# One low part of the next expert's gate weights, moved ahead of the scaling of finished rows

## The reference

```python
# each token goes to 2 of 32 experts; rows are sorted by expert, in blocks
def run_block(args):
    xb, e = args
    h = jax.nn.silu(xb @ w_gate[e]) * (xb @ w_up[e])     # 1024 -> 512
    return h @ w_down[e]                                  # 512 -> 1024
out = out.at[slot_tok].add(ys * slot_gate[:, None])
x = x + out
return rms_norm(x, final_g)        # x * rsqrt(mean(x*x) + eps) * g, row by row
```

## Time and profile before

| what | value |
| --- | --- |
| median of the runs | 2077.36 us (2075.55 to 2087.81, 3 runs) |
| the profiled execution, its own time | 2084.54 us |
| span of the profiled execution | 2082.6 us |
| granted clock over the span | 0.971 |
| PE busy | 1935.8 us, 93% |
| DVE busy | 1344.3 us, 65% |
| ACT busy | 1166.8 us, 56% |
| POOL busy | 868.4 us, 42% |

### The profile page before, as it was taken

How to read it: one execution, slowest core, us unless ns; L and a number is a source line. 1 busy time by engine, 2 the same in 40 slices (tenths; PEclk the granted TensorE clock), 3 DMA queues, 4 the chain that set the end, 5 groups by cost and what they waited for, 6 DMA issues and landing times. The chain is left out here.

```text
span 2082.6 us, 39849 instructions
## 1 busy us (share of the span) xinstructions
PE 1935.8 (93%) x12329; PEld 1646.0 (79%) x12330; DVE 1344.3 (65%) x2479; ACT 1166.8 (56%) x2436; POOL 868.4 (42%) x1044
## 2 busy tenths in 40 slices
PE   7999999979999999989999679899999999999996
PEld 6888888867777787878878568788888888788885
DVE  5333333339888888845656559766777777787764
ACT  4211111128888889853333248666666667686763
POOL 3332222213656644431332335445454345344544
PEclk9999999979999999989999889999999999999998
DMA  7433334375363543224543569968878978987852
GB/s 224 147 122 122 121 121 123 114 187 151 107 189 98 131 112 92 69 72 152 166 167 126 209 197 368 359 219 295 288 267 289 361 243 292 364 300 288 287 196 71
DMA packets 230803, 406.35 MB, mean 195 GB/s; under 512 B 31201, under 2 KB 169057, under 8 KB 206480
## 3 DMA queue, kind: packets, MB, share of 16 engines
q1 hardware_dynamic: 201328, 352.08, 49.7%
q0 software_dynamic: 29376, 53.03, 9.6%
HBM read 345.83 MB, written 111.15 MB: 219 GB/s over the span
## 5 line engine op out<-in xcount | busy, mean ns | idle before, releaser
L747 ACT ACTIVATE prob<-score,nmax 128x512 f32<-128x512 f32 (+3 forms) x464 | 264.4, 580 | 24.7 <-DVE nmax L897 24.1
L65 PE MATMUL proj<-w_in_lo,n1T_hi 128*128 128x512 f32 (+1 forms) x640 | 242.8, 379 | 3.5 <-DVE w_in_lo L250 3.4
L897 DVE TENSOR_REDUCE nmax<-score 128x2 f32<-128x1024 f32 (+3 forms) x232 | 212.5, 920 | 39.9 <-PE score L945 38.4
L66 PE MATMUL proj<-w_in_hi,n1T_lo 128*128 128x512 f32 (+1 forms) x640 | 237.3, 371 | 0.0
L67 PE MATMUL proj<-w_in_hi,n1T_hi 128*128 128x512 f32 (+1 forms) x640 | 237.1, 371 | 0.0
L812 POOL TENSOR_SCALAR prob<-prob,scale,lam 128x512 f32<-128x512 f32 (+3 forms) x168 | 139.1, 840 | 152.7 <-DVE scale L884 143.1
L1774 POOL DMA_INDIRECT acc_scratch<-y,own x47 | 143.9, 3062 | 96.7 <-ACT y L1955 79.7
L269 DVE TENSOR_TENSOR cosx<-proj,rope_sb 128x512 f32<-128x512 f32 (+1 forms) x64 | 37.9, 592 | 213.2 <-PE proj L67 213.2
L1978 DVE TENSOR_TENSOR wd_lo<-raw_pieces,wd_hi 128x1024 fp32r<-128x1024 f32 x128 | 148.2, 1217 | 7.5 <-ACT wd_hi L1962 7.5
L764 ACT COPY aT<-aT_ps 128x512 f32<-128x512 f32 (+3 forms) x232 | 122.6, 528 | 51.0 <-PE aT_ps L962 49.1
L1978 DVE TENSOR_TENSOR wg_lo<-raw_pieces,wg_hi 128x1024 fp32r<-128x1024 f32 x124 | 146.9, 1218 | 5.3 <-ACT wg_hi L1940 3.9
(11 more groups left out here) (305 smaller groups left out, 5532.9 us busy)
## 6 DMA issues: line engine op xcount, KB each, us to landing
raw_pieces<-in_w_down SPq DMA_DIRECT2D x64, 1024.0 KB, 9.7
raw_pieces<-in_w_gate SPq DMA_DIRECT2D x62, 1024.0 KB, 6.4
raw_pieces<-in_w_up SPq DMA_DIRECT2D x62, 1024.0 KB, 7.6
qk_scratch<-qkT SPq DMA_DIRECT2D x94, 256.0 KB, 2.4
xT_sb<-in_xT SPq DMA_DIRECT2D x16, 512.0 KB, 5.1
h<-in_x SPq DMA_DIRECT2D x16, 512.0 KB, 6.3
acc_scratch<-h SPq DMA_DIRECT2D x16, 512.0 KB, 3.0
n_scratch<-n SPq DMA_DIRECT2D x16, 512.0 KB, 5.5
```

Of the source, the lines that this page charges most:

```text
L65: pe.matmul(out, hi, w_lo, start=first, stop=False)
L66: pe.matmul(out, lo, w_hi, start=False, stop=False)
L747: act.activation(prob[:, n % RING, c, 0:w], score[:, n % BUFS, c, 0:w], ACT.Exp, bias=nmax[:, c, n:n + 1], accum_out=part[:, c, n:n + 1]). ...
L897: dve.tensor_reduce(nmax[:, :, n:n + 1], score[:, n % BUFS, :, 0:w], AX.X, ALU.max, negate=True).then_inc(max_ready, 1)
```

## The change

In a full block VectorE computes low part 3 between `hidden(b, 0)` and `normalize(b)` instead of behind `hidden(b, 1)`, and ScalarE computes high part 3 in front of `square(b)` instead of behind it. Nothing is added or removed.

```diff
@@ full_block on ScalarE
                     act.activation(hid[:, :], g_ps[:, :], ACT.Silu).then_inc(silu_ready, 1)
+                    highs(3)
                     square(b)
-                    highs(3, 4, 5)
+                    highs(4, 5)
                     copy_hT(b, 0)
@@ full_block on VectorE
                     hidden(b, 0)
+                    lows(3)
                     normalize(b)
                     split_hT(b, 0)
                     hidden(b, 1)
-                    lows(3, 4, 5)
+                    lows(4, 5)
                     split_hT(b, 1)
```

## The result

| | before | changed |
|---|---|---|
| median (9 runs each, side by side), us | 2077.36 (2072.88 to 2087.81) | 2091.85 (2081.46 to 2098.55) |
| ratio to before | | 1.006 [1.0036, 1.0084] |
| profiled execution: own time, span, granted clock | 2084.54, 2082.6, 0.971 | 2093.61, 2091.7, 0.966 |

The change made the kernel 0.6% slower: a small loss, within the 1% that I called no change, and outside the predicted range (2042 to 2087) on the slow side. The sign was wrong.

What follows compares the result with a forecast made beforehand. It took TensorE's waits in the expert stage as the bound; -27.4 - 5 + 11 + 9 = -12.4 us gave 2072.1 for the profiled execution and 2065 for the median (chance 0.40), range 2042 to 2087.

Steps and rivals of the forecast that it cites:

- What bounds the kernel: Expert stage: TensorE is busy 93% of the span, so only what it waits for is worth time.
- Part 1: Full blocks: TensorE's wait at the second half of the down product, in 30 blocks, goes, saving 27.4 us.
- Part 2: Full blocks with a late square: waits before the down product's first half shrink by 0.8 us or go; 5 us won.
- the full-block half of 5: Full blocks behind a full block: gathered rows come 1.5 us later against TensorE, giving 11 us back as first waits.
- Part 3: Relaxed full blocks: VectorE's scaling, up to 1.16 us later, uses up the slack; fetch_whole goes out about 0.8 us later.
- Part 4: GpSimd's var or rstd waits for low part 3's end, undoing most of Part 2 in seven or eight of ten blocks.
- Part 5, small blocks: Small blocks: late rows hold the square before ScalarE's last copy; TensorE waits in ten of 15, 9 us back.
- small blocks tip over: Rival, chance 0.10: squares in small blocks later than 4.5 us stall TensorE and lower its clock; 2093 to 2111 us.
- Nothing comes back: Rival, chance 0.27: the earlier gate load fills a DMA hole, gathered rows land sooner, nothing is given back; 2045 us.
- All of it comes back: Rival, chance 0.18: saturated DMA engines set the pace, the rows' chain stays 20.0 us; within 5 us of before, 2075.
- The low part isn't ready: Rival, chance 0.05: low part 3 waits for high part 3 behind a late Silu, delaying scaling and split; 2068 us.

Runs made afterwards that it cites:

- Experiment 5: The kernel before with low part 3 on VectorE between the split of the first half and the second product of gate and up; ratio 0.9954.
- experiment 1: The kernel before with only ScalarE's half of the change: high part 3 in front of the square, low part 3 where it was; ratio 0.9977.
- experiment 11: The changed kernel with SyncE's load of gate pieces 2 and 3 held back by two low parts; ratio 1.005.
- 2: The kernel before with only VectorE's half of the change: low part 3 in front of the scaling, high part 3 behind the square; ratio 1.013.
- 12: The changed kernel with low part 3 behind the scaling and the split of the first half instead of in front of the scaling; 2056.69 us, ratio 0.9855.
- 3: The changed kernel with the square in small blocks moved behind ScalarE's last copies; ratio 1.0001.
- 6: The changed kernel with GpSimd in full blocks issuing fetch_whole ahead of the gather of x; ratio 0.9889.
- experiment 10: The changed kernel with low part 6 ahead of VectorE's split of the next block's x; ratio 1.0037.
- 8: The kernel before with low part 3 behind the split of the first half and fetch_whole ahead of the gather of x; ratio 0.9859.
- 7: The kernel before with GpSimd in full blocks issuing fetch_whole ahead of the gather of x; ratio 0.9883.
- 9: The kernel before with high part 3 in front of the square and fetch_whole ahead of the gather of x; ratio 0.9869.
- 4: The kernel before with the square in small blocks moved behind ScalarE's last copies; ratio 1.0084.

## Why the prediction was wrong, point by point

- **What bounds the kernel**: right. All of the difference in the expert stage lies in TensorE's waits and their clock; the excess accounts for its 11.1 us to 0.1.
- **Part 1**: right in mechanism and size. All second waits are gone, the down product takes 5.58 us where it took 6.32. Over all 31 blocks the down products got 25.0 us shorter, against 27.4 predicted.
- **Part 2**: not borne out as a gain of its own. 17 first waits hold 19.9 us, where 16 held 13.1 (the ten behind a late square 11.5): the rows come later, and that covers the 0.8 us per block. Every full block that follows a full block now stands. The sum was off as well: of the ten, six and not five are below 0.8 us (3.3 us together) and four shrink by 0.8, which makes 6.5, and half of that is 3.2 and not 5. And the six waits behind a long store didn't stay, since the changed kernel has no such store. The second full block, relaxed before, is one of the new ones (VectorE and TensorE):

```profile
1249.80 1.28 DVE L1997 SCALAR_TENSOR_TENSOR final<-whole,rstd,gf_bc 128x1024 f32<-128x1024 f32 x1 [1.80 <-POOL rstd L1792]
```

```profile
1251.66 0.49 PE L65 MATMUL y_ps<-wd_lo,hT 128*128 128x512 f32 x1 [1.29 <-DVE hT L1990]
```

  Here TensorE stands 1.29 us for the split, in a block that had no first wait.
- **Parts 1, 2 and the full-block half of 5 together**: predicted -27.4 - 5 + 11 = -21.4, measured -18.0 (-25.0 in the down products, +7.0 in front of them, where -5 + 11 had been predicted). Off by 3.4.
- **Part 3: this step failed.** It said `fetch_whole` goes out "later by about 0.8 us". It went out 1.91 later. I had let part of the scaling's 1.16 vanish in "waiting anyway", and carried the rest along the chain as if only the scaling set it. I did not follow GpSimd's instructions behind the scaling to see which low parts they now fall onto: with the low part behind the scaling and the scaling unmoved, `fetch_whole` is 0.94 later (5), with the scaling 0.5 later and the low parts unmoved it isn't later at all (1). That the slack of relaxed blocks would just be used up was right: the down product starts at 6.76 in both.
- **Part 4** had the mechanism and sought it in the wrong place. `rstd` takes 0.57 us in relaxed blocks and its scaling isn't held by it; the hold falls on the copies and the indirect DMAs from the store on, and in all 14 relaxed blocks on a copy in front of it (`final_at`, 0.91 instead of 0.18), which delays nothing, because the store waits for the scaling anyway. The Trainium skill (SBUF — State Buffer, SBUF: two separate sides) names the pair of a VectorE operation with two SBUF inputs and a GpSimd operation that reads SBUF; the copies of 0.95 and 0.89 where they took 0.27 and 0.19 agree.
- **Part 5, small blocks**: this term was mis-sized, +9 predicted, **+29.1** measured. Two errors multiply: rows 2.65 us later against TensorE instead of 1.5 tip 12 blocks, not 10, and by 2.1 us of waiting on average (24.7 / 12), and each us of it costs 1.8 because of the clock; I had priced 0.9 per block, although the same prediction counted 3 us for each of the five blocks that stalled before (7.6 us of waiting).
- **The rival "small blocks tip over"**, held at 0.10 and 2093 to 2111, named this mechanism, and the time came out 1 us below its lower edge. I dismissed it because the rows "would have to land later than 3 us behind the present time", which I took to be out of reach. They did: the squares of the small blocks 9, 26 and 39 of the 47 moved from 2.44, 2.45 and 2.44 us after the gate product to 6.01, 5.64 and 6.29. 2.65 us of this are the later request; the other 0.5 to 1.2 are a later landing, and no run here shows its cause.
- **"Nothing comes back"** rested on an earlier load that fills the hole in the DMA engines. The hole was partly filled, at about the same place in the block (4.6 us after the gate product; in us, busy times, clock, DMA share, GB/s of the changed kernel; compare, 0.14):

```profile
1360.00:1362.00 2.00, 2.00 (x19) 2.00 (x19) 1.99 (x5) 1.47 (x3) 0.09 (x1) 1.00 0.46 78
1362.00:1364.00 2.00, 2.00 (x13) 1.70 (x12) 2.00 (x3) 1.02 (x1) 1.82 (x1) 1.00 0.87 365
```

  but the rows landed hardly sooner after their gather (9.2 us in the middle, 9.5 before), and in experiment 11, with the load held back, it is 9.2 too and the time is that of the change. The Trainium skill (DMA: Bandwidth & Descriptors, Queues, rings and completion order) has the engines take turns between queues packet by packet; I had set this against the rival, and these times don't contradict it.
- **"All of it comes back"** was right that the rows' chain limits, wrong that it would stop at zero: the chain itself got longer. **"The low part isn't ready"** did not happen in the relaxed blocks: low part 3 starts right behind the first product (1358.82 above, no idle time).

Shown: the VectorE half loses and the ScalarE half doesn't (1, 2); the place of the one low part decides the sign (12); the stalls of small blocks for the rows carry it (3), and they and the net loss vanish when the rows are asked for earlier, though a wait for x takes their place (6); the early load plays no part that shows (11). Not shown apart: how much of the 1.91 us costs time through the scaling and how much through GpSimd's held instructions, since experiment 10 only moved the hold. Experiment 5 puts the second alone at 0.94 us of lateness, and by experiment 1 the first 0.5 us of a later scaling adds none.

The fastest versions by their ratios are experiments 12 and 8, 2057 and 2050 us, 1.4 to 1.5% faster than before; 6, 7 and 9 lie within their intervals. Both at once was not tried.

## What to carry to other kernels

Filling an engine's idle time ahead of an operation that others wait for isn't free, even if the bounding engine doesn't feel it in that block: follow every step of the chain to the next transfer and see what it now runs beside, and compare the new lateness with the slack where the transfer is awaited, one block on. The same filler behind that operation took most of the same waits away here and kept the gain. Price a short stand of TensorE by what the blocks lose, not by the stand alone.

## What the runs showed of the hardware that I had not expected

- Indirect DMA issues on GpSimd that begin early in one of VectorE's low parts are held as the copies are: 1.84 and 1.88 us in the block shown where they took 1.03 and 1.04. In the changed kernel 32 of 48 stores and 31 of 47 `fetch_whole` took over 1.3 us, before 7 and 7. I had looked for this only in `var` and `rstd`.
- The granted clock was still 1.00 in the stand of 2.49 us and fell behind it, to 0.50 from 1526 to 1529, with TensorE busy again; over the 14 us around it is 0.88.
- The six accumulating stores of 7.5 us have no counterpart in the changed kernel, where they take 1.6 to 2.7 us. Such stores are in experiments 1, 4 and 5 too (1, 3 and 5 of them) and in no other. No run here shows the cause.
